# A hybrid attention and convolution step on one core: the norm weight arrives as a column, and the forget block is split

## The chip, the core and the metric

The kernel runs on one core of a Trainium2 chip. The core has five engines that run side by side, each with its own list of instructions: TensorE (PE in the profile, with PEld for its weight loads), VectorE (DVE), ScalarE (ACT), GpSimd (POOL) and SyncE (SP), which here only issues DMAs. The engines meet at semaphores. Everything is float32. The metric is the device time of one execution in microseconds (us); lower is better.

## The reference, cut to what matters

The reference is one inference step of one transformer-like layer for 1024 prompt tokens and 32 sample tokens. What the change touches is its very beginning:

```python
def rmsnorm(x, g):
    xf = x.astype(jnp.float32)
    y = xf * lax.rsqrt(jnp.mean(xf * xf, axis=-1, keepdims=True) + RMS_EPS)
    return (y * g.astype(jnp.float32)).astype(x.dtype)
...
    z = jnp.einsum('btd,de->bte', h, w_in)          # h = rmsnorm(x, norm_mix_pre)
    qa, ka, va, fa, qb, kb, vb, ga, gb = jnp.split(z, ...)
    logf = jax.nn.log_sigmoid((fa + fox_f_bias).astype(jnp.float32))
```

`g` is `norm_mix_pre`, a row of 1024 weights. `fa` are the 8 forget logits of each token. Two attention branches, their merge, and a convolutional feed-forward block follow, each a chain of large matrix products.

## The kernel before

The 1056 tokens lie in nine tiles of 128 rows (the last has 32). The first stage turns each tile t = 0 to 8 into a normalized, transposed and split one, and hands it from engine to engine:

- SP loads the tile into `xin` (512 KB each), in order, with the first weight slabs between them: `xin` 0, 1, 2, slab 0 (256 bytes for each of 1024 runs), `xin` 3, slab 1 (512-byte runs), `xin` 4 and so on. ACT issues two loads of its own first: `gbc`, the norm weight broadcast to all 128 partitions (512 KB), and `cst`, which holds the identity that transposes need (336 KB).
- ACT squares the tile and sums (L1789, "squares"). The program makes it wait for the squares of the tile before.
- POOL raises the mean square to -0.5 (L1031, `stat`, the tile's scale).
- DVE multiplies by the scale and by `gbc` into `hn` (L2437).
- PE transposes `hn` by eight products with the identity (L1241), four into one PSUM bank, four into the next.
- ACT rounds each bank to its high part `ht_h` (L1753, "highs", two for a tile), and DVE subtracts to the low part `ht_l` (L2407, "lows", two for a tile).

Between the tiles stand the first products. A product of this kernel is split in three: high by high, high by low, low by high (L1206 to L1208), over eight blocks of the inner dimension. The weights' own high and low parts are made by POOL in half slabs (L1045 high, L1051 low), which stand in POOL's list between the scales: the low part of slab 1's first half stands behind the scale of tile 4, and all later halves follow it, each with the scales of tiles 5 to 8 between. `dense_half(n, c, i)` is one half of slab n's product for token chunk c (352 tokens). The forget block `forget_dense(c)` (L1268) is slab 0's product. Its weight is 40 columns wide (high and low part side by side), so it takes 8 products with `ht_h` and 8 with `ht_l`.

Each engine's order is written out by hand. PE transposes tiles 0 to 3, runs `forget_dense(0)`, transposes tile 4, runs `dense_half(1, 0, 0)`, and goes on so through tile 7, where `dense_half(2, 0, 1)` stands. Tile 8 and `forget_dense(1)` and `(2)` follow. ACT takes the highs of tile t - 3 right before the squares of tile t. DVE takes the lows of tile t - 1 right behind `hn` of tile t. After this stage the kernel is one long run of such products.

## Time and profile before

| what | us |
|---|---|
| median of 3 runs | 1521.62 |
| lowest and highest run | 1519.12 and 1526.38 |
| profiled execution, its own time | 1519.1 |
| its span, first to last instruction | 1517.3 |
| PE busy in the span | 1484.6 (98%) |
| DVE, POOL, ACT busy | 1005.9, 614.9, 609.6 |
| first product or transpose starts at | 9.36 |

All durations below come from the one profiled execution. A timeline row gives the start, the duration, the engine, the line, the operation with output and inputs, how many instructions were merged, and in square brackets how long the engine sat idle before and what ended that. In a row of stretches the clock column is the granted TensorE clock as a share of 2.4 GHz, so 0.50 is 1.2 GHz.

### The profile page before, as it was taken

Reading aid. Unit: us, or ns where it says so; the run is one execution under the profiler, and the core shown is the slowest. Engines: PE = TensorE matmul, PEld = TensorE weight load, DVE = VectorE, ACT = ScalarE, POOL = GpSimd, SP = SyncE. Lnnn points to the kernel's source line nnn. Section 1 sums busy time; section 2 is a strip of 40 time slices with the busy share of each in tenths; the row PEclk is TensorE's granted clock in tenths of the full one; section 3 lists DMA queues with packets and bytes.
Section 4 is the critical chain, followed back from the end, with each engine's and each line's share of the span. In section 5 each row is a group of like instructions: output and inputs, shape, how many; then the busy total and the mean of one; then the engine's idle time right before and its main releaser. Section 6 shows DMA issues by size and latency. Waiting matters only on the chain.

```text
span 1517.3 us, 25684 instructions
## 1 busy us (share of the span) xinstructions
PE 1484.6 (98%) x9803; PEld 1393.7 (92%) x9803; DVE 1005.9 (66%) x1913; ACT 609.6 (40%) x1265; POOL 614.9 (41%) x403
## 2 busy tenths in 40 slices
PE   6999999999999999999999999999999999999996
PEld 5999999999998999899888999999999998778885
DVE  6976656676665377866456987655555556478986
ACT  5143534434343256655223343333233333444463
POOL 5522322223222313134222678888787880000104
PEclk9999999999999999999999999999999999999998
DMA  6232232122143611158321122222222229623558
GB/s 203 58 102 78 74 107 86 39 76 67 33 122 126 222 52 52 53 173 287 99 98 49 42 85 86 85 68 74 85 85 85 83 65 324 201 92 111 187 188 157
DMA packets 156474, 165.40 MB, mean 109 GB/s; under 512 B 14005, under 2 KB 121913, under 8 KB 156353
## 3 DMA queue, kind: packets, MB, share of 16 engines
q1 hardware_dynamic: 124297, 113.80, 24.1%
q10 hardware_dynamic: 30232, 46.69, 9.2%
q0 software_dynamic: 1824, 3.28, 1.6%
q8 instruction: 79, 1.29, 0.4%
q14 instruction: 42, 0.34, 0.1%
HBM read 125.56 MB, written 39.85 MB: 109 GB/s over the span
## 4 chain that ended last, share of the span: by engine, by line
PE 85%; DVE 9%; ACT 2%; DMA 1%; issue 1%; POOL 1%; SPq 1%; ACTq 0%; POOLq 0%; DVEq 0%
PE bank L1206 18%; PE bank L1208 17%; PE bank L1207 17%; PE bank L1214 6%; PE bank L1212 6%; PE bank L1213 6%; PE bank L1241 4%; PE bank L1350 2%; PE bank L1321 1%; PE bank L1320 1%; PE bank L1711 1%; PE bank L1713 1%; DVE conv L2955 1%; DVE p L2754 1%; DMA ysr<-d_y 1%
## 5 line engine op out<-in xcount | busy, mean ns | idle before, releaser
L1206 PE MATMUL bank<-ht_h,ring_h 128*128 128x352 f32 x816 | 269.1, 330 | 0.8 <-DVE vqn L2418 0.4
L1208 PE MATMUL bank<-ht_h,ring_l 128*128 128x352 f32 x816 | 262.7, 322 | 0.0
L1207 PE MATMUL bank<-ht_l,ring_h 128*128 128x352 f32 x816 | 261.9, 321 | 0.0
L994 POOL TENSOR_TENSOR ring_h<-raw,att 128x1024 fp32r<-128x1024 f32 x40 | 88.0, 2200 | 378.0 <-PE bank L1208 368.9
L1206 PE MATMUL bank<-m_h,ring_h 128*128 128x264 f32 x648 | 184.2, 284 | 1.1 <-DVE m_l L2998 1.0
L1207 PE MATMUL bank<-m_l,ring_h 128*128 128x264 f32 x648 | 184.2, 284 | 0.0
L1208 PE MATMUL bank<-m_h,ring_l 128*128 128x264 f32 x648 | 183.9, 284 | 0.0
L1206 PEld LDWEIGHTS bank<-ht_h,ring_h 128*128 128x128 f32 x816 | 153.2, 188 | 4.2 <-issue 1.8
L1207 PEld LDWEIGHTS bank<-ht_l,ring_h 128*128 128x128 f32 x816 | 153.9, 189 | 0.7
L1208 PEld LDWEIGHTS bank<-ht_h,ring_l 128*128 128x128 f32 x816 | 153.3, 188 | 0.0
L1206 PE MATMUL bank<-tb_h,ring_h 128*128 128x264 f32 x456 | 129.9, 285 | 0.0
L1208 PE MATMUL bank<-tb_h,ring_l 128*128 128x264 f32 x456 | 129.6, 284 | 0.0
L1207 PE MATMUL bank<-tb_l,ring_h 128*128 128x264 f32 x456 | 129.6, 284 | 0.0
L1206 PEld LDWEIGHTS bank<-m_h,ring_h 128*128 128x128 f32 x648 | 121.9, 188 | 1.6 <-DVE m_l L2998 1.3
L1208 PEld LDWEIGHTS bank<-m_h,ring_l 128*128 128x128 f32 x648 | 122.0, 188 | 0.0
L1207 PEld LDWEIGHTS bank<-m_l,ring_h 128*128 128x128 f32 x648 | 121.7, 188 | 0.0
L1214 PE MATMUL bank<-op_bh,op_al 128*128 128x512 f32 x308 | 120.3, 391 | 0.0
L1213 PE MATMUL bank<-op_bl,op_ah 128*128 128x512 f32 x308 | 120.2, 390 | 0.0
L1212 PE MATMUL bank<-op_bh,op_ah 128*128 128x512 f32 x308 | 120.0, 390 | 0.0
L995 POOL TENSOR_TENSOR ring_l<-raw,ring_h 128x1024 fp32r<-128x1024 f32 x40 | 109.8, 2744 | 3.1
L2581 DVE CUSTOM_DVE_ANT_0 ssb<-bank,negc 128x512 f32<-128x512 f32 (+2 forms) x96 | 50.8, 554 | 86.6 <-PE bank L1324 50.9
L1148 POOL TENSOR_TENSOR ring_l<-sw,ring_h 128x512 fp32r<-128x512 f32 x57 | 92.0, 1620 | 4.2 <-ACT ring_h L1753 4.2
(388 smaller groups left out, 3833.6 us busy)
## 6 DMA issues: line engine op xcount, KB each, us to landing
raw<-in_w_up SPq DMA_DIRECT2D x44, 512.0 KB, 3.9
raw<-in_w_in SPq DMA_DIRECT2D x34, 512.0 KB, 4.0
rb<-in_w_down SPq DMA_DIRECT2D x66, 256.0 KB, 2.9
d_y<-conv SPq DMA_DIRECT2D x22, 529.0 KB, 3.1
d_gate<-gst ACTq DMA_DIRECT2D x48, 176.0 KB, 1.9
a<-d_y SPq DMA_DIRECT2D x33, 256.0 KB, 5.5
ra<-d_y SPq DMA_DIRECT2D x33, 256.0 KB, 2.8
gm<-d_gate ACTq DMA_DIRECT2D x8, 528.0 KB, 4.8
```

What stands on the lines that cost most here:

```text
L994: order.link(nc.gpsimd.tensor_tensor(high, src, zero.to_broadcast(list(src.shape)), ALU.add))
L995: nc.gpsimd.tensor_tensor(low, src, high.bitcast(F32), ALU.subtract).then_inc(slab_split, 1)
L1148: nc.gpsimd.tensor_tensor(l, x, h.bitcast(F32), ALU.subtract).then_inc(w_ready, 1)
L1206: nc.tensor.matmul(out, wh, xh, start=start, stop=False, skip_group_check=onto)
L1207: nc.tensor.matmul(out, wh, xl, start=False, stop=False, skip_group_check=onto)
L1208: return nc.tensor.matmul(out, wl, xh, start=False, stop=stop, skip_group_check=onto)
L1212: nc.tensor.matmul(out, th, wh, start=start, stop=False, skip_group_check=onto)
L1213: nc.tensor.matmul(out, th, wl, start=False, stop=False, skip_group_check=onto)
L1214: return nc.tensor.matmul(out, tl, wh, start=False, stop=stop, skip_group_check=onto)
L1241: last = nc.tensor.transpose(o, i, ident[0:i.shape[0], 0:i.shape[0]])
L1350: nc.tensor.matmul(bank[7][:, o:SPAN], vhl[:, k, h, :], pt[:, k, o:SPAN], start=False, stop=False)
L2581: V.tensor_tensor_reduce(out=ssb[:, s % 2, o:o + w], in0=sbank(sc)[:, 0:w], in1=negc[:, h, o:o + w], scale=1.0, scalar=-3e38, op0=ALU.add, ...
```

## The change

Three edits, all in the first stage:

1. `gbc` is no longer loaded. A tile `gcol` takes the 1024 weights as one column for each block of 128 (partition p holds weights p, 128 + p, and so on), by a load of 1024 runs of 4 bytes that ACT issues behind `cst`. PE transposes each column, broadcast along the free dimension, by the identity (eight products into banks 0 and 1), ahead of all tiles. DVE copies the two banks to `gbc` ahead of the first `hn`.
2. ACT takes the highs of tile 2 (the third tile) ahead of the squares of tile 4 (the fifth) instead of behind them.
3. `forget_dense(0)` runs in two passes: the 8 products with `ht_h` ahead of tile 3's transposes, where they wait for the highs only, and the 8 with `ht_l` behind them. Chunks 1 and 2 keep their order; their first pass waits for highs and their second for lows.

```diff
@@ -156,6 +156,7 @@
     stat, _ = place("stat", [P, 64])
     cwt, _ = place("cwt", [P, 6, FT])
     tails, _ = place("tails", [P, 4, FT])
+    gcol, _ = place("gcol", [P, KT])
     qs, _ = place("qs", [P, 2 * PAIRS, DEC])
     smallf, _ = place("smallf", [P, 24])
     att, _ = place("att", [P, 64])
@@ -360,6 +361,7 @@
     sem = nc.alloc_semaphore
     ident_in = sem("ident_in")
     gbc_in = sem("gbc_in")
+    gbc_made = sem("gbc_made")
     setup_in = sem("setup_in")
     raw_in = [sem(f"raw_in{i}") for i in range(NRAW)]
     slab_split = sem("slab_split")
@@ -1243,6 +1245,12 @@
                 ti[0] += 1
 
             pe.wait_ge(ident_in, 16)
+            pe.wait_ge(gbc_in, 16)
+            for e in range(2):
+                for k in range(4):
+                    mm = nc.tensor.transpose(bank[e][:, P * k:P * k + P],
+                                             gcol[:, 4 * e + k:4 * e + k + 1].to_broadcast([P, P]), ident)
+                mm.then_inc(gbc_made, 1)
 
             def dense_half(n, c, i):
 
@@ -1257,27 +1265,33 @@
                 if i:
                     mm.then_inc(chunk_full, 1)
 
-            def forget_dense(c):
+            def forget_dense(c, high=True, low=True):
 
                 q = position(S_F, c)
-                pe.wait_ge(slab_split, S_F + 1)
-                pe.wait_ge(t_free, 6 * (c + 1))
-                wait_bank_free(pe, q)
-                for x in (ht_h, ht_l):
+                for x in (ht_h,) * high + (ht_l,) * low:
+                    if x is ht_h:
+                        pe.wait_ge(slab_split, S_F + 1)
+                        pe.wait_ge(t_high, 6 * (c + 1))
+                        wait_bank_free(pe, q)
+                    else:
+                        pe.wait_ge(t_free, 6 * (c + 1))
                     for k in range(KT):
                         mm = nc.tensor.matmul(bank[q % 3][0:FLOW + HEADS, 0:CH], ring_h[:, S_F, k, 0:FLOW + HEADS],
                                               x[:, k, CH * c:CH * c + CH], start=(x is ht_h and k == 0),
                                               stop=(x is ht_l and k == KT - 1))
-                mm.then_inc(chunk_full, 1)
+                if low:
+                    mm.then_inc(chunk_full, 1)
 
             for t in range(NT + 1):
+                if t == 3:
+                    forget_dense(0, low=False)
                 pe.wait_ge(h_rows, t + 1)
                 r = rows(t)
                 for e in range(2):
                     transposes(lambda b: [(b[:, P * k:P * k + r], hn[0:r, t % 2, P * (4 * e + k):P * (4 * e + k) + P])
                                           for k in range(4)])
                 if t == 3:
-                    forget_dense(0)
+                    forget_dense(0, high=False)
                 elif 4 <= t <= 7:
                     dense_half(1 + (t - 4) // 2, 0, (t - 4) % 2)
             forget_dense(1)
@@ -1753,8 +1767,9 @@
                 return nc.scalar.activation(out, in_, cp, scale=scale)
 
 
-            act.dma_start(gbc[:, :], norm_mix_pre.to_broadcast([P, D])).then_inc(gbc_in, 16)
             act.dma_start(cst[:, :], consts).then_inc(ident_in, 16)
+            with nc.allow_non_contiguous_dma(reason="one norm weight per partition"):
+                act.dma_start(gcol[:, :], norm_mix_pre.rearrange("a (k p) -> p (a k)", p=P)).then_inc(gbc_in, 16)
             def highs(i, outs):
 
                 act.wait_ge(t_full, i + 1)
@@ -1776,7 +1791,10 @@
                 copy(ls1[:, CH * c:CH * c + CH], bank[q % 3][FLOW:FLOW + HEADS, 0:CH]).then_inc(forget_low, 1)
 
             for t in range(NT + 4):
-                if t >= 3:
+                if t == 4:
+                    pre_high(1)
+                    pre_high(2)
+                elif t >= 3 and t != 5:
                     pre_high(t - 3)
                 if t == 7:
                     forget_lows(0)
@@ -2427,11 +2445,13 @@
             def early_chunk(dst, n, c):
                 copy_chunk(dst, position(n, c), c)
 
+            for e in range(2):
+                dve.wait_ge(gbc_made, e + 1)
+                order.mark(V.tensor_copy(gbc[:, 512 * e:512 * e + 512], bank[e][:, :]))
+            order.catch_up()
             for t in range(NT + 1):
                 r = rows(t)
                 dve.wait_ge(scale_ready, t + 1)
-                if t == 0:
-                    dve.wait_ge(gbc_in, 16)
 
                 wait(dve, t_full, 2 * (t - 1))
                 V.scalar_tensor_tensor(hn[0:r, t % 2, :], xin[0:r, t, 0:D], stat[0:r, 27 + t:28 + t], gbc[0:r, :],
```

ACT at the start of the program, before (`junk,stat` are the squares of one tile, `ht_h` the highs, `x_in4` the landing of tile 4):

```order
L1756 DMA gbc<-in_norm_mix_pre 128x1024
L1757 DMA cst<-in_consts 128x672
L1789 ACT_TABLE_LOAD [waits eps_in]
L1789 ACTIVATE junk,stat<-xin 128x1025 [waits x_in0]
L1789 ACTIVATE junk,stat<-xin 128x1025 [waits pre_sq,x_in1]
L1789 ACTIVATE junk,stat<-xin 128x1025 [waits pre_sq,x_in2]
L1753 ACTIVATE ht_h<-bank 128x4x128 [waits t_full] x2
L1789 ACTIVATE junk,stat<-xin 128x1025 [waits pre_sq,x_in3]
L1753 ACTIVATE ht_h<-bank 128x4x128 [waits t_full] x2
L1789 ACTIVATE junk,stat<-xin 128x1025 [waits pre_sq,x_in4]
L1753 ACTIVATE ht_h<-bank 128x4x128 [waits t_full] x2
L1789 ACTIVATE junk,stat<-xin 128x1025 [waits pre_sq,x_in5]
```

and now:

```order
L1770 DMA cst<-in_consts 128x672
L1772 DMA gcol<-in_norm_mix_pre 128x8x1
L1807 ACT_TABLE_LOAD [waits eps_in]
L1807 ACTIVATE junk,stat<-xin 128x1025 [waits x_in0]
L1807 ACTIVATE junk,stat<-xin 128x1025 [waits pre_sq,x_in1]
L1807 ACTIVATE junk,stat<-xin 128x1025 [waits pre_sq,x_in2]
L1767 ACTIVATE ht_h<-bank 128x4x128 [waits t_full] x2
L1807 ACTIVATE junk,stat<-xin 128x1025 [waits pre_sq,x_in3]
L1767 ACTIVATE ht_h<-bank 128x4x128 [waits t_full] x4
L1807 ACTIVATE junk,stat<-xin 128x1025 [waits pre_sq,x_in4]
L1807 ACTIVATE junk,stat<-xin 128x1025 [waits pre_sq,x_in5]
L1767 ACTIVATE ht_h<-bank 128x4x128 [waits t_full] x2
```

The load of `gbc` is gone and that of `gcol` stands behind `cst`; the squares of tile 4 moved behind the highs of tile 2.

PE from tile 3's transposes (banks 5 and 6) to tile 4's (banks 3 and 4), before (`hn` rows are transposes, 40x352 rows the forget block):

```order
L1241 MATMUL bank5<-cst_49,hn_83 128x128 [waits t_free,h_rows]
L1241 MATMUL bank5<-cst_49,hn_83 128x128 x3
L1241 MATMUL bank6<-cst_49,hn_83 128x128 [waits t_free]
L1241 MATMUL bank6<-cst_49,hn_83 128x128 x3
L1268 MATMUL bank0<-ht_h_61,ring_h_59 40x352 [waits t_free,slab_split]
L1268 MATMUL bank0<-ht_h_61,ring_h_59 40x352 x7
L1268 MATMUL bank0<-ht_l_62,ring_h_59 40x352 x8
L1241 MATMUL bank3<-cst_49,hn_83 128x128 [waits t_free,h_rows]
L1241 MATMUL bank3<-cst_49,hn_83 128x128 x3
L1241 MATMUL bank4<-cst_49,hn_83 128x128 [waits t_free]
L1241 MATMUL bank4<-cst_49,hn_83 128x128 x3
```

and now, at the same place, up to the end of tile 4's transposes:

```order
L1279 MATMUL bank0<-ht_h_62,ring_h_60 40x352 [waits t_high,slab_split]
L1279 MATMUL bank0<-ht_h_62,ring_h_60 40x352 x7
L1243 MATMUL bank5<-cst_49,hn_84 128x128 [waits t_free,h_rows]
L1243 MATMUL bank5<-cst_49,hn_84 128x128 x3
L1243 MATMUL bank6<-cst_49,hn_84 128x128 [waits t_free]
L1243 MATMUL bank6<-cst_49,hn_84 128x128 x3
L1279 MATMUL bank0<-ht_l_63,ring_h_60 40x352 [waits t_free]
L1279 MATMUL bank0<-ht_l_63,ring_h_60 40x352 x7
L1243 MATMUL bank3<-cst_49,hn_84 128x128 [waits t_free,h_rows]
L1243 MATMUL bank3<-cst_49,hn_84 128x128 x3
L1243 MATMUL bank4<-cst_49,hn_84 128x128 [waits t_free]
L1243 MATMUL bank4<-cst_49,hn_84 128x128 x3
```

The forget block's first eight products moved ahead of tile 3's transposes, with a wait on the highs (`t_high`) in place of the lows (`t_free`). At the very start of PE's list stand eight new transposes, of `gcol` into banks 0 and 1, which wait for both of ACT's loads.

DVE at the start of the program, now (before, `hn` was its first row, waiting for `gbc_in` and the scale):

```order
L2450 COPY gbc<-bank 128x512 [waits gbc_made] x2
L2457 SCALAR_TENSOR_TENSOR hn<-xin,stat,gbc 128x1024 [waits scale_ready,dve_seq]
L2457 SCALAR_TENSOR_TENSOR hn<-xin,stat,gbc 128x1024 [waits scale_ready]
L2425 TENSOR_TENSOR ht_l<-bank,ht_h 128x4x128 [waits t_high] x2
L2457 SCALAR_TENSOR_TENSOR hn<-xin,stat,gbc 128x1024 [waits t_full,scale_ready]
L2425 TENSOR_TENSOR ht_l<-bank,ht_h 128x4x128 [waits t_high] x2
```

Two copies from PSUM stand ahead of the first `hn`, and that waits for them (`dve_seq`). The instructions of POOL and SP stand as they did.

## Rows read from the trace of the kernel before

**Rows 1.** The page: the span, and each engine's busy time

```profile
span 1517.3 us, 25684 instructions
...
PE 1484.6 (98%) x9803; PEld 1393.7 (92%) x9803; DVE 1005.9 (66%) x1913; ACT 609.6 (40%) x1265; POOL 614.9 (41%) x403
```

**Rows 2.** PE's waits over the span: us in total, times, longest

```profile
PE bank L1241 <- DVE hn L2437: 12.0, 4, 9.4
...
PE bank L1206 <- POOL ring_l L1051: 0.3, 1, 0.3
```

**Rows 3.** Timeline of the first 20 us, all engines

```profile
7.93 1.28 DVE L2437 SCALAR_TENSOR_TENSOR hn<-xin,stat,gbc 128x1024 f32<-128x1024 f32 x1 [7.93 <-POOL stat L1031]
...
9.36 1.94 PE L1241 MATMUL bank<-cst,hn 128*128 128x128 f32 x8 [9.36 <-DVE hn L2437]
...
10.15 1.28 DVE L2437 SCALAR_TENSOR_TENSOR hn<-xin,stat,gbc 128x1024 f32<-128x1024 f32 x1 [0.93 <-POOL stat L1031]
...
11.46 1.29 DVE L2407 TENSOR_TENSOR ht_l<-bank,ht_h 128x512 fp32r<-128x512 f32 x2
...
12.67 1.27 DVE L2437 SCALAR_TENSOR_TENSOR hn<-xin,stat,gbc 128x1024 f32<-128x1024 f32 x1
...
15.29 1.06 ACT L1789 ACTIVATE junk<-xin 128x1025 f32<-128x1025 f32 x1 [0.94 <-DMA xin<-in_x_prompt]
...
16.34 1.06 ACT L1753 ACTIVATE ht_h<-bank 128x512 fp32r<-128x512 f32 x2
16.51 0.61 POOL L1031 TENSOR_TENSOR stat<-stat,att 128x1 f32<-128x1 f32 x1 [0.88 <-ACT junk L1789]
```

**Rows 4.** DMAs issued in the first 1.5 us: size, us from issue to landing

```profile
xin<-in_x_prompt SPq DMA_DIRECT2D x1, 512.0 KB, 5.4
gbc<-in_norm_mix_pre ACTq DMA_DIRECT2D x1, 512.0 KB, 5.5
...
cst<-in_consts ACTq DMA_DIRECT2D x1, 336.0 KB, 7.4
```

**Rows 5.** DMA queues from 718.5 to 719 us: packets, MB, share of 16 engines

```profile
q10 hardware_dynamic: 48, 0.18, 91.4%
q1 hardware_dynamic: 35, 0.02, 11.8%
```

**Rows 6.** DMA packets from 9 to 10 us

```profile
DMA packets 973, 0.32 MB, mean 317 GB/s; under 512 B 954, under 2 KB 954, under 8 KB 973
```

**Rows 7.** DMA packets from 78.3 to 78.55 us

```profile
DMA packets 451, 0.02 MB, mean 65 GB/s; under 512 B 447, under 2 KB 451, under 8 KB 451
```

**Rows 8.** Two stretches: engines' busy us, granted clock, DMA

```profile
13.90:15.20 1.30, 1.09 (x8) 0.86 (x8) 1.30 (x4) 0.45 (x1) 1.30 (x3) 1.00 1.02 406
...
16.20:19.60 3.40, 2.83 (x12) 2.47 (x13) 3.17 (x5) 3.40 (x9) 2.94 (x3) 0.51 1.07 342
```

**Rows 9.** Timeline of POOL, 18 to 31 us

```profile
18.52 1.35 POOL L1031 TENSOR_TENSOR stat<-stat,att 128x1 f32<-128x1 f32 x1
...
20.96 2.14 POOL L1051 TENSOR_TENSOR ring_l<-raw,ring_h 128x512 fp32r<-128x512 f32 x1
...
23.58 1.04 POOL L1045 TENSOR_TENSOR ring_h<-raw,att 128x512 fp32r<-128x512 f32 x1
24.95 1.16 POOL L1031 TENSOR_TENSOR stat<-stat,att 128x1 f32<-128x1 f32 x1 [0.33 <-ACT junk L1789]
...
27.33 2.23 POOL L1045 TENSOR_TENSOR ring_h<-raw,att 128x512 fp32r<-128x512 f32 x1
...
30.04 1.26 POOL L1051 TENSOR_TENSOR ring_l<-raw,ring_h 128x512 fp32r<-128x512 f32 x1
```

**Rows 10.** Timeline of PE around the forget block and its wait at 31

```profile
20.33 1.45 PE L1268 MATMUL bank<-ht_l,ring_h 128*40 128x352 f32 x8
...
22.41 0.41 PE L1206 MATMUL bank<-ht_h,ring_h 128*128 128x352 f32 x1
...
31.36 0.43 PE L1206 MATMUL bank<-ht_h,ring_h 128*128 128x352 f32 x1 [0.30 <-POOL ring_l L1051]
```


## The prediction

> **What bounds the kernel now.** I read the page first: PE is busy for 1484.6 of 1517.3 us [rows 1]. Then PE's waits over the whole span: the largest group by far is the transposes waiting for `hn`, 12.0 us in four waits [rows 2], all in the first 17 us. So the kernel is a long PE stream behind a short start, and what an edit of the start is worth is the time by which the stream begins earlier or later. Later waits of PE are short and hang on work that begins behind this stage, so a shift is passed on whole. The question is only where the shift is fixed.
>
> The timeline of the start tells that. Tile 0's `hn` begins at 7.93, released by POOL's scale; the second begins at 10.15 after 0.93 us of waiting for its scale; from then on DVE alternates `hn` (1.28) and a tile's lows (1.29) [rows 3]. The second row to see is the last wait: at 31.36 PE waits 0.30 us for POOL's low half of slab 2 [rows 2, 10]. PE's own list and POOL's list arrive there almost together. Both bound the stage: PE from tile 3's transposes on, and POOL from the scale of tile 4 at 16.51 [rows 3], through five scales and the half slabs, to 31.30, the end of its last `ring_l` [rows 9].
>
> **The load.** Tile 0 and `gbc`, 512 KB each, ran side by side and landed at 0.73 + 5.4 and + 5.5, so 6.1 and 6.2; `cst` landed at 1.18 + 7.4 = 8.6 [rows 4] (issue times 0.73 and 1.18 are the timeline's). Now `cst` (336 KB) runs beside tile 0: 176 KB less in front of both, at 317 GB/s [rows 6] about 0.5 us. I put both landings at 5.6. Tile 0's scale would then let `hn` begin at 7.4.
>
> But `hn` also needs the weight, and `gcol` is 1024 runs, 64 for each of 16 DMA engines. Which packets pass first when both queues are full? From 718.5 to 719 the ACT queue (4096-byte packets) and the SP queue (512-byte) moved 48 and 35 packets [rows 5]: near one to one, whatever the size. So each small packet of `gcol` waits for one packet of the other queue. A 4096-byte packet takes 0.91 x 0.5 x 16 / 46 = 0.16 us of an engine, counting 46 large ones in that row. Behind `cst` the SP queue holds tiles 1 and 2 (8 such packets for each engine and tile) and slab 0 (64 packets of 256 bytes). Slab 0's cost 16 / 954 = 0.017 us each [rows 6]. The nearest price for a 4-byte packet is that of a 32-byte one in a store, 0.25 x 16 / 441 = 0.009 us [rows 7]. Sum: 16 x (0.16 + 0.009) = 2.7 us for the first 16, then 48 x (0.017 + 0.009) = 1.25 us. `gcol` lands at 5.6 + 2.7 + 1.25 = 9.55, rather than with `cst`. The ends: at 0.004 us less or 0.02 us more for a packet, 9.3 to 10.8; the row has a store and this is a load, so I keep the high end wide.
>
> The Trainium skill ("DMA: Bandwidth & Descriptors", "Rules for kernel authors") speaks against this edit: a strided last dimension lowers to one descriptor per element, and it advises to rearrange. The store in the trace agrees as to the count, a packet for each run; no row here shows what a 4-byte load costs.
>
> **The broadcast.** Eight transposes of 128 x 128, as of tile 0, took 1.94 us [rows 3], the pace of TensorE's low level: eight of tile 2 took 1.09 at clock 1.00 [rows 8]. PE is idle until 9.55, so I take 1.94. Bank 1 is full at 11.5. Then DVE copies 128 x 512 from PSUM; the nearest row is a low of the same shape, 1.29 / 2 = 0.65 [rows 3]. The first copy lies beside the second four transposes, the second does not. `hn` of tile 0 begins at 12.3, against 7.93: **4.4 us later**. In other words the load that is 176 KB smaller saves 0.5 us of a path that no longer counts.
>
> **Given back.** DVE's wait of 0.93 us before the second `hn` goes, since all scales are ready. Against that, tile 0's transposes run at the low level and their highs come up to 0.6 us late for the lows. Third `hn` (tile 2): 12.67 - 7.93 = 4.74 before; 4.74 - 0.93 + 0.6 = 4.4 now, so it begins at 16.7 and ends at 18.0. This is +4.0.
>
> **Highs of tile 2 ahead of the squares of tile 4.** Before, the squares began at 15.29, released by tile 4's landing, and the highs followed at 16.34 [rows 3]. Now the squares wait for tile 2's transposes: 18.0 + 1.1 = 19.1 for the transposes, + 0.5 for the last high, + 1.2 for the squares. POOL's scale of tile 4 begins at 20.9, against 16.51: **+4.4**, of which 0.4 is this edit's own. Queued behind it on POOL are all half slabs but the first high. That the tiles land earlier is worth nothing then.
>
> **POOL's list.** From 16.51 it ran to 31.30 with waits of 0.33 for squares and some tenths of hand-overs [rows 9]. Moved by 4.4 less the 0.33, it ends at 35.4, and PE's product at 31.36 begins 4.0 us later. For the other end: POOL's instructions of one shape take 0.61 and 1.35, 1.16 (scales), 1.26 and 2.14 (`ring_l`), 1.04 and 2.23 (`ring_h`) [rows 3, 9]. The long ones lie beside an `hn` of DVE, which has the same four tiles in this stretch afterwards. If none were stretched, POOL would end 0.74 + 0.55 + 0.88 + 1.19 = 3.4 us sooner, and PE's own list would decide.
>
> **The forget block in two passes, and PE's list.** The first pass waits for tile 2's highs, 19.6, and takes 1.3 to 20.9 at full clock (8 products took 1.45 with their tail, 1.3 to the next [rows 10]). `hn` of tile 3 ends at 18.0 + 1.29 + 1.3 = 20.6; its transposes run to 22.0, tile 2's lows too, and the second pass ends at 23.3, when `hn` of tile 4 (20.6 + 1.29 + 1.3 = 23.2) is there too. Transposes to 24.4, then the first dense half, at 22.41 before [rows 10]: **+2.0**. The split does its work: 1.3 us of PE hide in DVE's time, and a stretch at clock 0.51 from 16.2 to 19.6, in which PE worked 2.83 us [rows 8], now falls where PE has less to do. Without these two, PE would be +4 as well. At the low level all through, the first pass and one tile more would cost 1 to 2 us here, which POOL's list still hides.
>
> **The sum.** PE at the product behind the last half slab: the larger of +2.0 (PE) and +4.0 (POOL). Between the ends I take **+3.4**, nearer to POOL's, because the four `hn` that stretch it are still there. The profiled execution took 1519.1 and would take 1522.5. It lies 2.5 us under the median of 1521.6, and the same shift gives a median of **1525.0**.
>
> **Rivals.**
> A. The column lands early: its small packets pass in one turn. Then it is there with `cst` at about 5.8, the eight transposes and the copy end at 8.5, and `hn` begins 0.5 us later than before. POOL's list gives +0.5 to 0 and PE's up to -2: the total is -1.5 to +1, a time of 1521.4. Rows 5 speak against it. The Trainium skill states a rule that would bring it about ("DMA: Bandwidth & Descriptors", "Queues, rings and completion order"): engines go round the queues by packets of up to 64 descriptors, and 64 is what each engine holds of `gcol`. By that rule the sum is this rival's; the near-equal counts of rows 5 are for the other.
> B. 4-byte loads are dear: the kernel becomes slower by over 0.5%. The place is the wait of PE's first transpose. A delay of 7.6 us at POOL's list needs `gcol` at 13.2 or later; 64 packets in 13.2 - 5.6 = 7.6 us, less 2.6 for the large ones and 0.8 for slab 0's 48, leave 0.065 us for each. From there it decides. Were each as dear as a 4096-byte one (0.16, the upper bound), it would land at 19.3 and the time be about 1535. For it: no load of 4-byte runs is in the rows. Against: 32 bytes cost 0.009 and 256 bytes 0.017.
> C. The delay is there and does not reach the end, because POOL's stretched instructions shrink and the clock is full from 16 us on: +0.9 to +2, a time of 1523.
> D. The low level holds PE for longer, so the first dense halves run at it: +5 to +7, a time of 1527.5.
>
> **Chances.** Forecast (+2 to +4.8) 0.50; A 0.17; C 0.15; D and a `gcol` between 10.8 and 13.2 together 0.10; B 0.08. Runs of the kernel before differ by 7 us, so a median of three carries 2 us of its own. The range leaves out B's far part and the lowest corner of A: 1519.5 to 1530.0. About 0.5% (7.6 us) is what a measurement can tell from no change: faster (under 1514.0) only with A's low end and a lucky draw, 0.02; slower (over 1529.2) for B and a part of D, 0.11; the rest, 0.87, is no change.
>
> **What would show it.** In the profile after: the landing of `gcol` (8 us after its issue), the first `hn` at 12.3, the squares of tile 4 released by highs rather than a DMA, POOL's scale of tile 4 at 20.9, PE waiting for `ring_l` before the dense halves of slab 2 for 1 to 2.5 us in all, the first dense half at 24.4. A first `hn` near 8.5 means A; over 16, B. A gain is possible only if it begins before 8.

## The result, and the profile after

| kernel | median us | lowest to highest | runs |
|---|---|---|---|
| before | 1521.19 | 1519.12 to 1526.38 | 17 |
| after | 1524.27 | 1521.88 to 1526.20 | 17 |

The ratio is 1.0019, with a 95% interval of 1.0013 to 1.0026: the change costs 3.1 us (2.0 to 4.0). That is within the 0.5% that was called no change, yet the interval excludes zero. The profiled execution of after took 1524.0, that of before 1519.1. The second is the fastest of its 17 runs.

The page of after: the span, and each engine's busy time, as in [rows 1].

```profile
span 1522.2 us, 25702 instructions
...
PE 1488.3 (98%) x9811; PEld 1396.8 (92%) x9811; DVE 1009.4 (66%) x1915; ACT 609.5 (40%) x1265; POOL 613.1 (40%) x403
```

PE's waits of after over the whole span (us in total, times, longest). The wait for the first `hn` in [rows 2] is now one for the column, and the wait for POOL's `ring_l` is about as short as it was.

```profile
PE bank L1251 <- DMA gcol<-in_norm_mix_pre: 9.3, 1, 9.3
...
PE bank L1243 <- DVE hn L2457: 3.0, 2, 2.1
...
PE bank L1208 <- POOL ring_l L1053: 0.4, 1, 0.4
```

The loads that ACT issues, in after: size, and us from issue to landing. `cst` landed at 0.74 + 4.8 = 5.5 and `gcol` at 1.19 + 8.0 = 9.2. Under them stand the DMA queues in a quarter of a microsecond of that wait, 7.75 to 8.0 us: q1 is SP's queue, which moves slab 0 (256-byte runs), q10 is ACT's, which moves the column (4-byte runs).

```profile
cst<-in_consts ACTq DMA_DIRECT2D x1, 336.0 KB, 4.8
gcol<-in_norm_mix_pre ACTq DMA_DIRECT2D x1, 4.0 KB, 8.0
```

```profile
q1 hardware_dynamic: 199, 0.05, 89.5%
q10 hardware_dynamic: 201, 0.00, 45.2%
```

The packets pass one for one. It is so beside a tile's 4096-byte packets too, 29 to 29 from 6.25 to 6.5 us. In steps of 0.01 us from 6.44 to 6.92 the column's counts repeat every 0.16 us, 16 in each such stretch, one for each engine; so the turn is a single packet and not a batch. A 4-byte packet has an engine for 0.25 x 16 x 0.452 / 201 = 0.009 us.

The timeline of after, from the column to PE's last wait for POOL in this stage. These rows answer to [rows 3, 9, 10].

```profile
9.34 1.94 PE L1251 MATMUL bank<-cst,gcol 128*128 128x128 f32 x8 [9.34 <-DMA gcol<-in_norm_mix_pre]
...
11.32 0.69 DVE L2450 COPY gbc<-bank 128x512 f32<-128x512 f32 x1 [0.16 <-PE bank L1251]
...
12.05 2.48 DVE L2457 SCALAR_TENSOR_TENSOR hn<-xin,stat,gbc 128x1024 f32<-128x1024 f32 x2
...
16.63 1.28 DVE L2457 SCALAR_TENSOR_TENSOR hn<-xin,stat,gbc 128x1024 f32<-128x1024 f32 x1
...
17.96 1.97 PE L1243 MATMUL bank<-cst,hn 128*128 128x128 f32 x8 [0.90 <-DVE hn L2457]
...
20.46 1.05 ACT L1807 ACTIVATE junk<-xin 128x1025 f32<-128x1025 f32 x1
...
20.71 2.54 PE L1279 MATMUL bank<-ht_h,ring_h 128*40 128x352 f32 x8 [0.78 <-ACT ht_h L1767]
...
21.68 0.55 POOL L1033 TENSOR_TENSOR stat<-stat,att 128x1 f32<-128x1 f32 x1 [2.08 <-ACT junk L1807]
...
24.61 2.26 PE L1279 MATMUL bank<-ht_l,ring_h 128*40 128x352 f32 x8
...
27.49 0.41 PE L1208 MATMUL bank<-ht_h,ring_h 128*128 128x352 f32 x1
...
35.18 1.26 POOL L1053 TENSOR_TENSOR ring_l<-raw,ring_h 128x512 fp32r<-128x512 f32 x1
36.50 0.43 PE L1208 MATMUL bank<-ht_h,ring_h 128*128 128x352 f32 x1 [0.38 <-POOL ring_l L1053]
```

The reader is to see three things. The first `hn` begins at 12.05 instead of 7.93, and the column alone holds it. POOL's scale of tile 4 begins at 21.68 instead of 16.51 (+5.2), and from there to the end of its last `ring_l` POOL takes 14.76 us, before 14.79: of this span nothing is given back. The product behind that half slab begins at 36.50 instead of 31.36, **5.1 us later**. The total is 3.1 later. So the document has two questions: what makes the 5.1, and where 2 us of it went.

### The profile page after: what moved, and what is told of

It is laid out like the page before. It is cut to its first block, busy times and chain, and to the rows that moved or that the text cites. A ratio compares the mean times of both kernels' runs of the same rounds, so it can differ in the third digit from the quotient of the medians.

```text
span 1522.2 us, 25702 instructions
## 1 busy us (share of the span) xinstructions
PE 1488.3 (98%) x9811; PEld 1396.8 (92%) x9811; DVE 1009.4 (66%) x1915; ACT 609.5 (40%) x1265; POOL 613.1 (40%) x403
## 4 chain that ended last, share of the span: by engine, by line
PE 83%; DVE 10%; DMA 2%; ACT 2%; POOL 1%; issue 1%; ACTq 0%; POOLq 0%; DVEq 0%
PE bank L1208 17%; PE bank L1210 17%; PE bank L1209 16%; PE bank L1214 6%; PE bank L1216 6%; PE bank L1215 6%; PE bank L1243 5%; PE bank L1364 2%; PE bank L1335 1%; PE bank L1334 1%; DMA gate<-d_gate 1%; PE bank L1725 1%; PE bank L1727 1%; PE bank L1279 1%; DVE conv L2975 1%
## 5 line engine op out<-in xcount | busy, mean ns | idle before, releaser
L996 POOL TENSOR_TENSOR ring_h<-raw,att 128x1024 fp32r<-128x1024 f32 x40 | 84.7, 2116 | 378.4 <-PE bank L1210 370.0
```

The source lines that it names most:

```text
L996: order.link(nc.gpsimd.tensor_tensor(high, src, zero.to_broadcast(list(src.shape)), ALU.add))
```

## The experiments

Each kernel is after with one edit, unless said otherwise. "The product" is PE's product behind POOL's last half slab of the first stage (31.36 before, 36.50 after). Medians are shown beside the median of before from the same batch.

### The column alone (e1), and the other two edits alone (e2)

e1 takes edits 2 and 3 back:

```diff
-                if t == 3:
-                    forget_dense(0, low=False)
...
-                    forget_dense(0, high=False)
+                    forget_dense(0)
...
-                if t == 4:
-                    pre_high(1)
-                    pre_high(2)
-                elif t >= 3 and t != 5:
+                if t >= 3:
```

> Only the first edit (column load, eight transposes, two copies); the highs of tile 2 and the forget block stand as before. Theory T (the late first hn sets the shift): first hn near 12.05 as in the changed kernel, scale of tile 4 about 4 us later than before's 16.51, and the forget block's 2.6 us are back on PE's path: 1524.5 to 1526.5, as slow as the changed kernel or slower. Rival R (the two order edits cost the time, by the new wait on highs and the later squares of tile 4): 1521 to 1522, no slower than before.

Measured: 1523.76 against 1520.21, ratio 1.0020 (1.0011 to 1.0029). e2 takes the column back and keeps the two orders:

```diff
+            act.dma_start(gbc[:, :], norm_mix_pre.to_broadcast([P, D])).then_inc(gbc_in, 16)
             act.dma_start(cst[:, :], consts).then_inc(ident_in, 16)
-            with nc.allow_non_contiguous_dma(reason="one norm weight per partition"):
-                act.dma_start(gcol[:, :], ...).then_inc(gbc_in, 16)
```

> Only the second and third edits; gbc is loaded as before. Theory T: first hn at 7.9; the squares of tile 4 start some 0.5 us later, POOL's list ends 0 to 0.5 us later, PE's own list is 1.3 us shorter: 1520.5 to 1521.8, not to be told from before. Rival R: the full loss, 1523.5 to 1525.

Measured: 1520.05 against 1520.21, ratio 0.9998 (0.9989 to 1.0006). The timeline of e1 (POOL's scales of tiles 4 and 7, and the product), then of e2 (the scale of tile 4, and the product):

```profile
19.43 1.52 POOL L1033 TENSOR_TENSOR stat<-stat,att 128x1 f32<-128x1 f32 x1
...
29.54 0.83 POOL L1033 TENSOR_TENSOR stat<-stat,att 128x1 f32<-128x1 f32 x1 [1.10 <-ACT junk L1802]
...
35.95 0.43 PE L1208 MATMUL bank<-ht_h,ring_h 128*128 128x352 f32 x1 [0.32 <-POOL ring_l L1053]
```

```profile
17.61 0.55 POOL L1033 TENSOR_TENSOR stat<-stat,att 128x1 f32<-128x1 f32 x1 [2.05 <-ACT junk L1800]
...
32.31 0.43 PE L1208 MATMUL bank<-ht_h,ring_h 128*128 128x352 f32 x1 [0.82 <-POOL ring_l L1053]
```

The whole cost is the column's: 1.0020 with it alone, 1.0019 with all three edits. In e2 the scale of tile 4 moves from 16.51 to 17.61 and the product by 0.95, but no change of the total can be measured. Most of that 1.1 is not the order of highs and squares itself: tile 2's transposes took 1.94 us in this execution and 1.09 in before's, and the squares now wait for them.

Beside the late column the two edits have larger prices, which nearly cancel. In e1 the scale of tile 4 begins at 19.43, 2.25 us ahead of after's, since its squares do not wait for tile 2's transposes. But from there to the end of the last `ring_l` POOL takes 16.5 us, where it takes 14.65 to 14.8 in before's first profile and in all ten profiles of after, e2, e3, e4, e5, e7, e8 and e9 (b_again: 15.1). It waits 1.10 us for the squares of tile 7, which ACT takes behind the highs of tile 4, and those wait for transposes that stand behind the unsplit forget block (they begin at 26.21). So the order of highs and squares costs 2.25 us at the scale, the split forget block saves most of it again, and the product differs by 0.55.

### The same column, issued first (e3)

SP issues it ahead of tile 0, so that it has no packet of another load to take turns with:

```diff
+                sp.dma_start(gcol[:, :], norm_mix_pre.rearrange("a (k p) -> p (a k)", p=P)).then_inc(gbc_in, 16)
...
             act.dma_start(cst[:, :], consts).then_inc(ident_in, 16)
-                act.dma_start(gcol[:, :], norm_mix_pre.rearrange("a (k p) -> p (a k)", p=P)).then_inc(gbc_in, 16)
```

> The changed kernel with the column load issued by SP ahead of tile 0 instead of by ACT behind cst. Theory T (the column was late because each of its packets took turns with a packet of the tiles, not because 4-byte packets are dear): it costs 64 packets of 0.009 us, 0.6 us, ahead of tile 0 and has landed when cst has; PE's eight transposes start near 5.8, the first hn near 8.5: 1520.5 to 1522. Rival P (a load of 4-byte runs is slow wherever it stands): it lands past 8 and delays tile 0 with it, 1524 or more.

Measured: 1518.19 against 1520.21, ratio 0.9985 (0.9977 to 0.9994). The landing of the column, then the timeline:

```profile
gcol<-in_norm_mix_pre SPq DMA_DIRECT2D x1, 4.0 KB, 3.9
```

```profile
4.74 1.94 PE L1253 MATMUL bank<-cst,gcol 128*128 128x128 f32 x8 [4.74 <-DMA gcol<-in_norm_mix_pre]
...
8.40 1.28 DVE L2457 SCALAR_TENSOR_TENSOR hn<-xin,stat,gbc 128x1024 f32<-128x1024 f32 x1 [1.00 <-POOL stat L1035]
...
32.84 0.43 PE L1210 MATMUL bank<-ht_h,ring_h 128*128 128x352 f32 x1 [0.57 <-POOL ring_l L1055]
```

1024 runs of 4 bytes land 3.9 us after the issue, against 8.0 behind `cst`. So the runs themselves are cheap, and the place is dear. This speaks for the turns and against the rival that 4-byte loads are dear wherever they stand. But something does not fit: in this profile the first `hn` begins 0.5 and the product 1.5 us later than before, and still the kernel is faster than before.

### A busy PE, and POOL's order, at the late start (e4, e6)

e4 adds 14 transposes of the identity, which nothing reads, ahead of those of the column:

```diff
             pe.wait_ge(ident_in, 16)
+            for i in range(14):
+                nc.tensor.transpose(bank[7][:, P * (i % 4):P * (i % 4) + P], ident, ident)
             pe.wait_ge(gbc_in, 16)
```

> The changed kernel with 14 more transposes of the identity into bank 7, which nothing uses then, between the waits for cst and for the column, where PE is idle. Theory C (TensorE's low level until 26 us added 2 to 3 us to PE's list and 0.9 us to the path to POOL's scale of tile 4): tile 2's transposes take 1.1 instead of 1.97 and the forget block's passes 1.3 instead of 2.1 in the profile, and the median falls by 0.7 to 2 us, to 1522.3 to 1523.6. Rival (POOL's list alone sets the shift, or the level does not depend on this work): 1524 to 1524.6.

Measured: 1523.80 against 1520.21, ratio 1.0020 (1.0011 to 1.0029). The view by stretches of e4 (bounds; us; busy us of PE, PEld, DVE, ACT and POOL; granted clock; DMA share and GB/s):

```profile
10.00:14.00 4.00, 1.89 (x14) 1.54 (x12) 3.66 (x4) 0.27 (x1) 0.63 (x2) 1.00 1.07 386
14.00:24.00 10.00, 8.42 (x36) 6.56 (x35) 9.22 (x11) 6.88 (x14) 5.99 (x7) 0.50 0.58 184
```

The clock was granted in full before and was back at 1.2 GHz from 14 to 24 us, after four microseconds in which PE was busy for 1.89. The transposes of tile 2 took 1.97 and the forget block's first pass 2.54, as in after. So this kernel does not test what a full clock in this stretch is worth; it shows only that work ahead of a gap did not keep the level through the gap. (Its product begins at 35.43, 1.1 us sooner than after's, as its first `hn` begins at 11.70 and its third 1.1 us sooner; the median does not show that either.) In after's own profile the clock column reads 1.00 there, but the same durations stand in its rows (1.97, 2.54, 2.26), and eight transposes at a clock of 1.00 took 1.09 [rows 8]. I go by the durations.

e6 puts the low half slab ahead of the scale of tile 4 in POOL's list, to use the 2.08 us in which POOL waits there:

```diff
-            pre_scale(4)
             half_low(1, 0)
+            pre_scale(4)
```

> The changed kernel with POOL's low half of slab 1 (1.28 us) ahead of the scale of tile 4, in the 2.08 us in which POOL waits for the squares of tile 4. If POOL's list alone sets the shift: it ends 1.3 us sooner and the median falls by 1 to 1.3, to 1523. If PE's list is level with it (the profile after shows PE waiting only 0.38 for the last half slab): PE's wait goes and the median falls by 0 to 0.5, to 1523.7 to 1524.3.

Measured: 1523.95 against 1520.77, ratio 1.0019 (1.0010 to 1.0028). The timeline of e6:

```profile
19.58 2.15 POOL L1053 TENSOR_TENSOR ring_l<-raw,ring_h 128x512 fp32r<-128x512 f32 x1
...
34.96 0.43 PE L1208 MATMUL bank<-ht_h,ring_h 128*128 128x352 f32 x1 [0.78 <-POOL ring_l L1053]
```

The half slab filled the gap, was stretched to 2.15 beside an `hn` of DVE, and the product begins 1.5 us sooner than in after. A part of that is not the order's: tile 2's transposes took 1.09 us in this execution, in after's 1.97. The median did not follow, 3.2 us over before against 3.1. The two intervals leave about 1.7 us of room between the kernels, so this does not prove that the 1.5 is lost.

### Another way to the same `gbc` (e5), and a busy PE at the early start (e7, e8)

e5 loads the weight as one row of 4096 bytes into one partition, first of ACT's loads, and PE spreads it by two products with a row of ones, which DVE sets:

```diff
+            act.dma_start(grow[:, :], norm_mix_pre).then_inc(gbc_in, 16)
             act.dma_start(cst[:, :], consts).then_inc(ident_in, 16)
...
-                for k in range(4):
-                    mm = nc.tensor.transpose(bank[e][:, P * k:P * k + P],
-                                             gcol[:, 4 * e + k:4 * e + k + 1].to_broadcast([P, P]), ident)
-                mm.then_inc(gbc_made, 1)
+                nc.tensor.matmul(bank[e][:, :], ones1[:, :], grow[:, 512 * e:512 * e + 512], start=True, stop=True
+                                 ).then_inc(gbc_made, 1)
```

> The changed kernel with the norm weight loaded as one row of 4 KB into one partition (one packet, first on ACT's queue), and broadcast by two products of a row of ones (1 x 128) with it, instead of the column load and eight transposes. Theory T (what counts is when the first hn can start): the row has landed by 3, the products end near 6.5, the copies by 7.3, and the first hn starts with its scale at 7.2 to 7.5; 1517.5 to 1519.5, faster than before by 1 to 3 us. Rival F (taking gbc's 512 KB away is worth nothing and the column-first version was faster by another cause): 1520 or more.

Measured: 1519.62 against 1520.77, ratio 0.9994 (0.9985 to 1.0002). The timeline of e5:

```profile
2.25 3.75 PE L1252 MATMUL bank<-grow,ones 1*128 1x512 f32 x4 [2.25 <-DMA grow<-in_norm_mix_pre]
...
30.35 0.43 PE L1210 MATMUL bank<-ht_h,ring_h 128*128 128x352 f32 x1 [0.81 <-POOL ring_l L1055]
```

The product begins 1.0 us sooner than before, the median is 1.15 lower, and the interval still holds 1.

e7 is e3 with 23 transposes of the identity that nothing reads: 4 ahead of the column's, 12 and 4 ahead of those of tiles 0 and 2, and 3 ahead of the forget block's first pass:

```diff
+            idle_work(4)
             pe.wait_ge(gbc_in, 16)
...
             for t in range(NT + 1):
+                idle_work({0: 12, 2: 4, 3: 3}.get(t, 0))
```

> The column-first kernel with idle PE time of the first 17 us filled by 23 transposes of the identity into bank 7 (4 ahead of the column's, 12 ahead of tile 0, 4 ahead of tile 2, 3 ahead of the forget block). Theory C (PE falls to its low level because it idles between the tiles, and this costs the stage): the granted level stays full from 10 us on, tile 2's transposes take 1.1, the forget passes 1.3 each, and the median falls by 1 to 2 us below the column-first kernel's 1518.2 (0.9985 of before). Rival (the level does not follow, or POOL's list bounds and nothing is gained): within 0.5 us of the column-first kernel.

Measured: 1517.49 against 1520.77, ratio 0.9976 (0.9966 to 0.9986). Its timeline: the transposes of tile 2 are at the pace of 2.4 GHz, and the product stands where before's does.

```profile
13.77 1.09 PE L1245 MATMUL bank<-cst,hn 128*128 128x128 f32 x8 [0.95 <-DVE hn L2464]
...
31.36 0.43 PE L1210 MATMUL bank<-ht_h,ring_h 128*128 128x352 f32 x1 [0.81 <-POOL ring_l L1055]
```

To learn whether the extra work counts, I ran e7 and e3 again side by side, and gave e5 the same treatment (e8: two more products of ones behind the first two, 4 transposes ahead of tile 2 and 3 ahead of the forget block).

> The same kernel as e7 (column first, 23 idle transposes), in 5 rounds beside e3. Theory W: 0.5 to 1.5 us below e3 in the same batch, ratio 0.9970 to 0.9985. Theory N: equal to e3 within 0.3 us; the earlier difference of the two ratios (0.9976 and 0.9985) was scatter of the runs.

Measured: 1517.26 against 1520.94, ratio 0.9975 (0.9966 to 0.9984).

> The same kernel as e3 (the column's load first on SP's queue), in 5 rounds beside e7. Both theories: faster than before by 1.2 to 2.5 us, ratio 0.9983 to 0.9992. If it comes out at 1.000 or above, the place of the column's load saves only what it had cost, and nothing more.

Measured: 1517.77 against 1520.94, ratio 0.9983 (0.9974 to 0.9992). Both repeat to 0.0002. e7 lies under e3 both times, by 0.5 us within the second batch, and the intervals overlap: a gain of the busy PE is likely and not shown.

> The row version (one 4-KB row, product with ones), and PE kept busy by two more ones-products (512 wide) before cst lands and by 4 and 3 extra transposes ahead of tiles 2 and 3. Theory W: a full clock in the first stage shortens it, because late highs stretch the chain ACT - POOL too: the fourth scale's successor (tile 4) starts at 14.5 to 15.2 against 15.64 in e5, and the median falls 0.7 to 1.5 us below e5's ratio of 0.9994, to 0.9985 to 0.9990 (about 1519). Theory N: POOL's list alone bounds the stage, whatever PE's clock: the ratio stays at 0.999 to 1.000. Theory X: the extra products cost time where PE's list bounds: over 1.0003.

Measured: 1521.97 against 1520.94, ratio 1.0013 (1.0004 to 1.0023). Here the extra work costs instead of bringing any: e5's median lay 1.15 us under before's, e8's lies 1.0 over it. The second pair of ones-products holds PE from 5.81 to 9.4, tile 0's transposes begin at 9.36, 1.2 us later than in e5, and the product, 31.84, is 1.5 later. So e8's expectation under theory X came true, by extra work that stood in the way.

### What the fast kernels have in common (b_again, e9)

> The kernel before once more, for a second profile. If the full level from 12.8 to 16.2 in the first profile was this execution's alone, the second one shows tile 2's transposes at 1.9 us, the forget block at up to 5 us and the product behind the last half slab at 32 to 33.5 instead of 31.36. If the shape of the kernel fixes it, the same times as in the first, to 0.3 us.

One more execution of the kernel before: 1521.43 in total, 2.3 us more than in its first profile, with the product at 31.6, 0.25 later. So its start repeats to a few tenths, and most of the difference between these two executions arises behind it.

That does not hold for every kernel. e3's product begins at 32.84 in one execution and at 31.57 in the other. Tile 2's transposes and the scale of tile 4, in e3 and then in e3 again:

```profile
14.32 1.97 PE L1245 MATMUL bank<-cst,hn 128*128 128x128 f32 x8 [0.87 <-DVE hn L2457]
...
18.03 0.55 POOL L1035 TENSOR_TENSOR stat<-stat,att 128x1 f32<-128x1 f32 x1 [2.08 <-ACT junk L1807]
```

```profile
13.83 1.10 PE L1245 MATMUL bank<-cst,hn 128*128 128x128 f32 x8 [1.01 <-DVE hn L2457]
...
16.72 0.55 POOL L1035 TENSOR_TENSOR stat<-stat,att 128x1 f32<-128x1 f32 x1 [1.26 <-ACT junk L1807]
```

By these durations the same kernel meets tile 2 once at 1.2 GHz and once at 2.4. Of the 1.27 us at the product 0.48 stood already at the first `hn` (8.40 and 7.92); the other 0.8 comes with the transposes, through the squares and the scale of tile 4. This is the number that e4 could not give. It also means that a shift of the product by up to 1.3 us between two kernels with one profile each can be the execution's.

I then set the profiles of all kernels beside each other by PE's waits, which stand in each of them at the same places of the list. Starts in us, read from their timelines. "p, 2nd" is PE's second wait for DVE's `p` behind 600 us, with its length in the next column; "m_l" is its wait for DVE's `m_l` (the low part of a later stage's input) near 900; "end" is the span.

| kernel | product | p, 2nd | its wait | m_l | end | ratio |
|---|---|---|---|---|---|---|
| before | 31.4 | 618.9 | 2.26 | 896.2 | 1517.3 | 1 |
| b_again | 31.6 | 620.0 | 2.27 | 898.9 | 1519.6 | 1 |
| after | 36.5 | 624.2 | 2.26 | 902.2 | 1522.2 | 1.0019 |
| e5 | 30.4 | 618.1 | 2.25 | 896.2 | 1516.7 | 0.9994 |
| e3 | 32.8 | 619.1 | 0.74 | 896.8 | 1516.7 | 0.9985 |
| e3 again | 31.6 | 617.9 | 0.77 | 895.2 | 1514.8 | 0.9983 |
| e7 | 31.4 | 617.6 | 0.78 | 897.1 | 1516.8 | 0.9976 |
| e7 again | 31.8 | 618.4 | 0.77 | 895.8 | 1515.6 | 0.9975 |

The kernels that the table leaves out (e1, e2, e4, e6, e8) have the long wait, 2.26 or 2.27.

From the product to the next wait at 573 us (`kwt`) it is 542.0 us in before and 542.1 in after: the shift of the start is passed on whole, as predicted. Then comes a place that has nothing to do with the first stage. PE waits for DVE's `p`, for 2.26 us in before and after and for 0.8 in all four profiles of e3 and e7. The timeline around it, before, and then e3 again (`p` is the matrix of attention weights, `ot_l` the low part of the attention's output, `ring_h` and `ring_l` the high and low part of a weight slab):

```profile
610.42 1.06 ACT L1753 ACTIVATE ring_h<-raw 128x1024 fp32r<-128x1024 f32 x1 [0.46 <-ACT gst L1753]
...
611.65 2.45 POOL L1088 TENSOR_TENSOR ring_l<-raw,ring_h 128x1024 fp32r<-128x1024 f32 x1 [3.08 <-ACT ring_h L1753]
...
611.87 2.37 DVE L2825 TENSOR_TENSOR ot_l<-o,ot_h 128x128 fp32r<-128x128 f32 x1
...
618.93 1.09 PE L1241 MATMUL bank<-cst,p 128*128 128x128 f32 x8 [2.26 <-DVE p L2754]
```

```profile
611.12 1.06 ACT L1769 ACTIVATE ring_h<-raw 128x1024 fp32r<-128x1024 f32 x1 [0.74 <-PE bank L1212]
...
612.29 0.29 DVE L2845 TENSOR_TENSOR ot_l<-o,ot_h 128x128 fp32r<-128x128 f32 x1
612.35 2.49 POOL L1092 TENSOR_TENSOR ring_l<-raw,ring_h 128x1024 fp32r<-128x1024 f32 x1 [3.36 <-ACT ring_h L1769]
...
617.85 1.09 PE L1245 MATMUL bank<-cst,p 128*128 128x128 f32 x8 [0.77 <-DVE p L2774]
```

Before, POOL's `ring_l` starts 0.22 us ahead of DVE's `ot_l`, and that small instruction takes 2.37 us and ends with POOL's. In e3 POOL starts 0.06 behind it, and the same instruction takes 0.29. The Trainium skill ("SBUF — State Buffer", "SBUF: two separate sides") says that the two engines share a pair of ports under an exclusive lock, held for a whole instruction by whichever came first, where DVE's instruction has two inputs in SBUF. `ot_l` has, and 2.37 against 0.29 agrees.

What decides who is first is ACT: ahead of `ring_h` it sits idle for 0.46 us before and 0.74 in e3. The DMA queues label some packets "instruction". Before, one of q14 passed between 608 and 609, some 2 us ahead of this `ring_h`; in e3 again it passed between 611 and 612, half a microsecond behind its start. The row of q14 from 608 to 609 us before, and then from 611 to 612 in e3 again (packets, MB, share of 16 engines):

```profile
q14 instruction: 1, 0.01, 3.3%
```

```profile
q14 instruction: 1, 0.01, 3.2%
```

In the nine profiles of the other kernels (after, b_again, e1, e2, e4, e5, e6 and e8 beside before) it stands 2 us ahead, counted in steps of 0.5 us, in the four of e3 and e7 half a microsecond behind. Those two kernels issue one DMA less from ACT's list at the start. e9 puts one back: e3, with 32 bytes more to load into a spare tile that nothing uses.

```diff
             act.dma_start(cst[:, :], consts).then_inc(ident_in, 16)
+            act.dma_start(spare[:, :], norm_mix_pre[0:1, 0:8]).then_inc(spare_in, 16)
...
                     dve.wait_ge(ident_in, 16)
+                    dve.wait_ge(spare_in, 16)
```

> The question is why e3 and e7 run 2 to 3.5 us under before although their product behind the last half slab (PE at 31 us) starts no earlier. In all four of their profiles ACT sits idle for 0.74 us ahead of one ring_h near 611 us, in the profiles of the other kernels for 0.46; POOL's ring_l behind it then starts just after DVE's ot_l instead of just ahead of it, DVE's ot_l takes 0.29 instead of 2.4 us, and PE's wait for p near 618 us is 0.8 instead of 2.3. They alone issue one DMA less on ACT's list. This kernel is e3 with one small DMA put back on ACT's list behind cst (eight weights to a spare tile that nothing reads; DVE waits for it at tile 8). Theory L (ACT's list decides: where the instructions behind one DMA more or less stand): ACT's idle time returns to 0.46, DVE's ot_l to 2.4, the wait for p near 618 to 2.3, and the median is 1.3 to 1.7 us above e3's (ratio 0.9990 to 0.9998, against 0.9983 and 0.9985). Theory S (the earlier start or SP's list decides): all three stay as in e3, ratio 0.998 to 0.9988. Both: first hn and PE at 31 us as in e3, within 0.5 us or so.

Measured: 1521.20 against 1520.49, ratio 1.0002 (0.9993 to 1.0011). The timeline, and the q14 packet between 609.5 and 610.5:

```profile
611.83 1.06 ACT L1771 ACTIVATE ring_h<-raw 128x1024 fp32r<-128x1024 f32 x1 [0.46 <-ACT gst L1771]
...
613.06 2.45 POOL L1094 TENSOR_TENSOR ring_l<-raw,ring_h 128x1024 fp32r<-128x1024 f32 x1 [3.08 <-ACT ring_h L1771]
...
613.29 2.37 DVE L2849 TENSOR_TENSOR ot_l<-o,ot_h 128x128 fp32r<-128x128 f32 x1
```

```profile
q14 instruction: 1, 0.01, 1.9%
```

The idle time is back at 0.46, `ot_l` at 2.37, PE's wait near 620 at 2.26, and with them the gain is gone. One DMA more or less on ACT's list, 600 us ahead of the place, decides which engine wins there. (e9 also adds a wait to DVE's list. But e3 and after have the same list on DVE, and e3 and e9 the same on SP: only ACT's list differs in both pairs.) That the packets carry ACT's code, and that their moving past these instructions makes the idle time, is an inference from these thirteen profiles and e9's; no run moved the packet alone.

The ratio rose by 0.0017 to 0.0019, 2.6 to 2.9 us, and the wait itself accounts for 1.5. e9's product begins at 32.58, between e3's two, so the first stage does not explain the rest. A part of the rest may stand right behind it. In b_again and in e6 the clock was granted at about half for 3.4 us just after this long wait (0.51 from 621.2 to 624.6; 0.56 from 624.0 to 627.4), and the way to the next wait for `p` took 22.5 us instead of 21.0. That happened in two of the ten profiles with the long wait and in none of the four with the short one. It is argued, not shown.

## Why the prediction came true, and where it did not

**The landing of the column: right.** Predicted 9.55, measured 9.2; by the count of [rows 5] the packets would pass one for one, and 201 to 199 did. A pair of a 4-byte and a 256-byte packet took 0.25 x 16 / 200 = 0.020 us of an engine where the working had 0.026, since their times overlap (the two shares add up to 135%); over 48 pairs that is 0.3 us, about the difference. `cst` and tile 0 were put at 5.6; `cst` landed at 5.5. The Trainium skill's rule of packets with up to 64 descriptors ("DMA: Bandwidth & Descriptors", "Queues, rings and completion order") would have let the column pass in one turn, at its upper end; the trace does not show that here. Rival A falls with it. The Trainium skill's advice against a descriptor for each element ("DMA: Bandwidth & Descriptors", "Rules for kernel authors") was right about this placing (e1: +0.20%), though e3 shows that the same descriptors at the head of a queue need not cost.

**The price of a 4-byte packet: right.** 0.009 us, the value taken from the 32-byte stores of [rows 7]. That sum took the engines as fully busy; with the queue's own share there, 82%, a store packet has an engine for 0.0074. Rival B (0.065 or more) falls.

**Transposes, copies, first `hn`: right.** 1.94, 0.69, and 12.05 where 12.3 was predicted. The third `hn`: 16.63 against 16.7.

**The scale of tile 4: too small.** Predicted 20.9 (+4.4), measured 21.68 (+5.2). The term that failed is the one for tile 2's transposes: I took 1.1 us, since at that time of before's profile the clock was full, and they took 1.97. I had said that tile 0's would be at the low level and did not carry it on; in e3 the level at this place is not even the same in two executions (1.97 and 1.10). The second wrong term is "of which 0.4 is this edit's own": beside e1 the order of highs and squares costs 2.25 us here, because the squares of tile 4 now wait for those transposes, while without it (e1) the scale is only 2.9 us later than before.

**POOL's list: the wrong end for the sum.** I took +3.4 between +2.0 and +4.0, and so let 0.6 us of POOL's stretched work go. From the scale of tile 4 POOL took 14.76 us against 14.79: nothing shrank. **PE's list** was put at +2.0 (24.4) and came at 27.49, +5.1, since the passes of the forget block took 2.54 and 2.26 rather than 1.3 each and the transposes between them ran slow too. The working allowed 1 to 2 us for the low level on this list; the list came 3.1 later than its 24.4. So the sign "PE waiting for `ring_l` for 1 to 2.5 us" failed: PE waited 0.4, as both lists came late together. This is rival D's mechanism, and the low end of its size (+5 to +7) at the product, where it was given 0.10 together with a late column.

**The total: right in size, partly for the wrong reason.** At the product the shift is +5.1, not +3.4. It is still +4.9 in the two profiled executions (1524.0 less 1519.1), and +2.5 against b_again. The medians differ by 3.1. The step that failed is "the same shift gives the median": the profiled execution of before lay 2.1 us under its median, that of after 0.3. b_again shows where one execution of before took longer than that profile: 0.9 us more up to 573 us behind the product, and 1.5 in the stretch with the low clock near 622. Why a kernel that starts 5 us later shows less of it on average stays open. A part can be chance: after was profiled once, and e3's product came 1.3 us apart in two executions. So the total came out within 0.3 us of the forecast shift by two misses of opposite sign, 1.7 too little at the product and 2.0 too much behind it; that nearness is luck.

**The two other edits: near nothing in sum, at other prices than given.** The order of highs and squares was priced at 0.4 and costs 2.25 at the scale of tile 4 (after against e1). The split pass was to keep PE at +2, and PE came at +5.1. Without both (e1) the product is 0.55 us sooner than with them and the median the same.

**The chances.** "No change" had 0.87, and the measured 0.19%, with an interval that ends at 0.26%, lies well inside it. The case that came, by its place at the product, is a mixture of the forecast and of D.

## What to carry to other kernels

A load of tiny runs costs what stands in the other queues beside it: count its packets per engine and price each with the packet that it takes turns with, then move it to where there is none (here 3.9 us instead of 8.0, and from 0.19% slower than before to level with it: e3 itself was 0.15 and 0.17% faster, but e9, which loads the column in the same way, has nothing of that left). When the total moves by 1 to 3 us in 1500, profile each kernel more than once and line up the waits of several profiles of both kernels before believing in a cause: here 1.5 us of an apparent gain of the start, of 2.0 in one batch of runs and 3.2 in the other, was made 580 us later, by which of two engines began an instruction first, and the rest went with it in e9. The fastest kernel measured is e7, 1517.3 to 1517.5 (0.9975, 0.9976); its gain over before is at least partly that accident, which another edit of ACT's list can undo.

## What the runs showed of the hardware that was not expected

- A DVE instruction of 0.29 us takes 2.37 when a POOL instruction of 2.45 starts 0.22 us ahead of it, and 0.29 when that starts 0.06 behind. A shift of 0.28 us decides 1.5 us of PE's time.
- One DMA more on ACT's list moves a packet labelled "instruction" by some 2.5 us relative to ACT's work 600 us later, and ACT's idle time ahead of it by 0.28 us (four profiles against ten).
- 4-byte and 256-byte packets take turns one for one (201 to 199 in 0.25 us), and a 4-byte one has its engine for 0.009 us.
- The same eight transposes in the same kernel took 1.97 us in one execution and 1.10 in the other, and the product behind followed by 0.8 us (e3).
- Two products with one row of ones (1 x 128 by 1 x 512, float32; four instructions in the trace) spread a 4096-byte row over 128 partitions in 3.75 us; the row was there 1.5 us after its issue at 0.73.
- In e4 the clock went from full to half at 14 us, after a stretch in which PE was busy for 1.89 of 4 us, and stayed there to 24 us with PE busy for 8.42 of 10.
